# A hybrid encoder layer with a mixture of experts: bias fetches spread over the projection copies, w_ada units moved, and the last residual folded into the expert loop

## The chip, the cores and the metric

The program runs on one core of one Trainium2 chip. The metric is device time in microseconds (us) for one execution. Engines: TensorE (PE, matrix products; PEld its weight loads), VectorE (DVE), ScalarE (ACT), GpSimd (POOL), and the sync engine (SP), which here only issues DMAs. Every engine runs its own instruction list in order and waits on semaphores.

## The reference, cut to what matters

There are two groups of tokens, 256 prompt tokens and 32 sample tokens, and one layer:

```python
mod = jax.nn.silu(c) @ w_ada + b_ada                 # per group, 6 vectors of 1024
sh1, sc1, g1, sh2, sc2, g2 = jnp.split(mod[:, None, :], 6, axis=-1)
mix, state = mixer(x * (1.0 + sc1) + sh1)            # w_in projection, three head groups, w_out
x = layer_norm(DEEPNORM_ALPHA * x + g1 * mix, ln_g[0], ln_b[0])
ffn = moe_ffn(x * (1.0 + sc2) + sh2, w_router, b_router, w_e_in, b_e_in, w_e_out, b_e_out)
x = layer_norm(DEEPNORM_ALPHA * x + g2 * ffn, ln_g[1], ln_b[1])
```

`mixer` projects with `w_in` (1024 x 2048) into queries and keys of attention groups A and B, their values, and the two halves of a gated convolution (width 31, then LayerNorm and swish). Attention logits get a bias taken from a table by relative position. `moe_ffn` sends each token to 4 of 32 experts; each expert has 8 MB of `w_e_in` and 4 MB of `w_e_out` in f32, so the experts' weights are 384 MB. `DEEPNORM_ALPHA` is 2 ** 0.25.

## The kernel before, in words

All tokens lie in three tiles: `t` = 0 and 1 hold 128 prompt rows each, `t` = 2 the 32 sample rows, which for row-wise work are spread over 128 partitions as quarters of 256 columns (`x1q`).

**Front.** SP loads `w_ada` (six vectors, "pairs" 0 to 5, each in two halves, so twelve "units" of 2 MB) through a ring of four slots, and `w_in` behind the first four units. A unit from 4 on reuses a slot once TensorE has passed an earlier unit (`ada_done`). TensorE transposes `x`, does units 0 to 3 (`ada(u)`, L1429), then sixteen projection jobs, in the order gg0, ga0, gg1, ga1 (convolution), k0, k1, q0, q1, qb0 to qb3, kb, v0, v1, v2 (L1549, L1544, L1524, L1529). The jobs use two PSUM banks in turn, so job n waits until ScalarE has copied job n-2 out (`proj_used`). Table `ADA_AFTER` says behind which job each remaining `w_ada` unit is multiplied. Behind kb come the transposes of the convolution's output (`conv_rows`), behind v0 those of the new keys (three, L1478), the cached keys (L1486, L1490) and the convolution state (L1496). All transposes share two banks: transpose job j waits until VectorE has copied job j-2 (`tr_used`). VectorE meanwhile runs the convolution (L1006, L1010), its statistics (L1020), `add_mod` (L962, adds `b_ada` to a finished pair) and the copies (L1046). ScalarE writes finished pairs to DRAM (`store_mod`, L667), from where they are read back as rows.

The attention bias is built by GpSimd as a small table, stored by ScalarE into `ext_dram`, and fetched from there by ten DMAs that ScalarE issues in a row, before its first projection copy (L657 to L662; copy L675).

**Attention, output projection, LayerNorm, router** follow (logits L1576, exponentials L747, w_out L1660).

**Experts.** Tokens of an expert are taken in blocks of 32 slots; 51 blocks occur here. For each block TensorE gathers the token rows by one-hot products (L1773, L1774), multiplies with `w_e_in` (L1793), transposes, multiplies with `w_e_out` (L1822, semaphore `S2`), and adds the gated result of the block before to the sums in PSUM (`comb` and bank 7; `combine(0..2)`, L1756 and L1752). `combine(0)` of a block stands behind the gathers of the next. VectorE makes the one-hot picks (L1339, L1287 to L1291) and the activation (L1298 to L1306); ScalarE copies the second product to `outb` (L895) for `combine`. SP streams 1 MB pieces of expert weights (L415, L418) into a ring of 20 slots, each as soon as the product that used it has passed. Experts 0 and 1 are written out in line; experts 2 to 31 are a loop `Fori(0, 6)` on TensorE whose body holds five experts, each with an inner loop over its blocks. VectorE, ScalarE and SP have loops of their own over the same experts.

**End.** VectorE waits for the last `combine`, multiplies the sums with `g2` (L1365), adds `ALPHA` times `x1` (L1366; GpSimd has completed `x1` long before, L599 to L606, `x1_ready`), and does the last LayerNorm (L1371 to L1381). `g2` rows and the LayerNorm rows are loaded by SP behind the last expert weights.

## Time and profile before

| | us |
|---|---|
| runs of the kernel | 1264.98, 1255.98, 1263.4 (median 1263.4) |
| the profiled execution | 1256.61 |
| span of its trace | 1254.6 |
| TensorE busy in it | 1024.4 (82%) |
| VectorE busy | 317.2 (25%) |
| ScalarE busy | 179.4 (14%) |
| GpSimd busy | 64.5 (5%) |
| moved by DMA | 454.26 MB, 362 GB/s in the mean |

The profiled execution lies 6.8 us below the median of the runs, and its span 2.0 us below its own time. Busy shares are averages over stages with different limits; what a stage waits for is read from the rows of that stage.

### The profile page before, as it was taken

The numbers are of one execution on the slowest core, as the hardware profiler recorded it, in microseconds if no ns is written. First come the engines' busy times: TensorE is split into PE (matmuls) and PEld (weight loads), VectorE is DVE, ScalarE is ACT, GpSimd is POOL, SyncE is SP. The second block draws the span as 40 slices with busy tenths as digits, with TensorE's granted clock in tenths as the row PEclk, the third lists the DMA queues.
The fourth block names the chain that finished last, engine by engine and source line by source line (L and its number), as shares of the span: only waits on it lengthen the run. The fifth ranks groups of instructions, "written<-read, shape, count | busy, mean of one in ns | idle before, by whom it ended". The sixth has DMA issues, their size and how long they took to land.

```text
span 1254.6 us, 30804 instructions
## 1 busy us (share of the span) xinstructions
PE 1024.4 (82%) x12329; PEld 480.6 (38%) x12330; DVE 317.2 (25%) x1020; ACT 179.4 (14%) x522; POOL 64.5 (5%) x142
## 2 busy tenths in 40 slices
PE   2799897898989779779789968997878997876872
PEld 1556654344434324224334424442333442332431
DVE  0297556322213111102121211121121121211215
ACT  0101434211101101001011101111110110100110
POOL 1830000000051000000000000000000000000000
PEclk9999899899989879879899989998998998888996
DMA  9995875699999999997997997099799999999994
GB/s 338 338 337 219 219 291 202 262 421 419 422 420 421 419 421 421 421 421 312 420 421 321 421 420 293 32 422 420 332 410 420 376 378 420 422 419 421 421 420 149
DMA packets 77729, 454.26 MB, mean 362 GB/s; under 512 B 9060, under 2 KB 16446, under 8 KB 28426
## 3 DMA queue, kind: packets, MB, share of 16 engines
q1 hardware_dynamic: 73412, 448.53, 88.1%
q10 hardware_dynamic: 4229, 4.41, 1.1%
...
## 4 chain that ended last, share of the span: by engine, by line
PE 40%; DMA 25%; SPq 22%; DVE 7%; issue 5%; ACT 1%; DVEq 0%
DMA w<-in_w_e_out 24%; PE bank L1793 15%; SPq L415 10%; PE bank L1822 8%; SPq L418 7%; PE bank L1773 3%; SPq L396 3%; PE comb L1756 2%; PE bank L1660 1%; PE comb L1660 1%; PE bank L1810 1%; PE bank L1786 1%; DVE mt L1306 1%; DVE mt L1302 1%; DVE mt L1298 1%
## 5 line engine op out<-in xcount | busy, mean ns | idle before, releaser
L1793 PE MATMUL bank<-w,mt 128*32 128x512 f32 x3264 | 397.1, 630 | 47.6 <-DMA w<-in_w_e_in 47.6
L1822 PE MATMUL bank<-w,mt 128*32 128x256 f32 x3264 | 199.0, 389 | 48.5 <-DMA w<-in_w_e_out 34.0
L1793 PEld LDWEIGHTS bank<-w,mt 128*32 128x32 f32 x3264 | 96.7, 114 | 307.9 <-issue 212.7
L1298 DVE TENSOR_SCALAR mt<-bank 128x256 f32<-128x256 f32 x51 | 21.6, 424 | 698.8 <-PE bank L1793 698.8
L1822 PEld LDWEIGHTS bank<-w,mt 128*32 128x32 f32 x3264 | 98.6, 111 | 131.2 <-DMA w<-in_w_e_out 51.3
L1773 PE MATMUL bank<-pick,hb 128*128 128x32 bf16 x2448 | 79.6, 180 | 52.6 <-issue 52.3
L1773 PEld LDWEIGHTS bank<-pick,hb 128*128 128x128 bf16 x2448 | 75.3, 98 | 76.9 <-issue 76.5
L886 ACT ACTIVATE mt<-mt 128x256 f32<-128x256 f32 x51 | 21.3, 417 | 500.1 <-DVE mt L1298 500.1
L1756 PE MATMUL comb<-mt,gpickT 32*128 32x256 f32 x816 | 82.0, 476 | 0.5 <-ACT mt L895 0.5
L1774 PE MATMUL bank<-pick,hb 96*128 96x32 bf16 x408 | 72.8, 179 | 0.0
L1756 PEld LDWEIGHTS comb<-mt,gpickT 32*128 32x128 f32 x816 | 35.9, 206 | 51.3 <-issue 48.1
L895 ACT ACTIVATE mt<-bank 128x256 f32<-128x256 f32 x51 | 19.6, 384 | 237.6 <-PE bank L1822 237.6
L1774 PEld LDWEIGHTS bank<-pick,hb 96*128 96x128 bf16 x408 | 40.1, 98 | 0.0
L1810 PE MATMUL bank<-ident,mt 128*128 128x128 f32 x102 | 25.1, 328 | 16.0 <-DVE mt L1306 16.0
L1752 PE MATMUL bank<-mt,gpickT 128*128 128x256 f32 x102 | 38.1, 457 | 0.0
L1010 DVE SCALAR_TENSOR_TENSOR w<-w,cwT 128x318 f32<-128x318 f32 x60 | 36.7, 612 | 2.3 <-DVE mt L962 0.2
L1289 DVE TENSOR_SCALAR gpick<-iota,rkc,gtc 128x128 f32 (+1 forms) x102 | 34.6, 380 | 0.0
L1339 DVE TENSOR_SCALAR pick<-iota,rkc 128x32 bf16 x150 | 27.2, 246 | 20.1 <-DVE gtc L1327 10.8
L888 ACT ACTIVATE gpickT<-bank 128x384 f32<-128x384 f32 x51 | 25.0, 491 | 39.9 <-PE bank L1806 39.9
L1549 PE MATMUL comb<-mt,w 128*128 128x288 f32 x80 | 22.7, 439 | 5.9 <-ACT w L675 3.8
...
L1810 PEld LDWEIGHTS bank<-ident,mt 128*128 128x128 f32 x102 | 16.1, 206 | 26.4 <-DVE mt L1306 26.3
...
## 6 DMA issues: line engine op xcount, KB each, us to landing
w<-in_w_e_in SPq DMA_DIRECT2D x256, 1024.0 KB, 26.0
w<-in_w_e_out SPq DMA_DIRECT2D x128, 1024.0 KB, 21.5
...
```

Of the source, the lines that this page charges most:

```text
L396: sp.dma_start(win[:, :, a:b], wi[:, :, a:b]).then_inc(ld_win[piece], 16)
L415: sp.dma_start(slot[s], src).then_inc(ld_slot[s], 16)
L418: sp.dma_start(slot[s], src).then_inc(ld_slot[s], 16)
L1010: link(v.scalar_tensor_tensor(out=yconv[:, c, :], in0=uext[:, c, w:w + Y_LEN], scalar=cwT[:, c, w:w + 1], in1=yconv[:, c, :], op0=ALU.mult ...
L1289: v.tensor_scalar(gpick[:, t, :, :], ids, rkc[:, t, :], gtc[:, t, :], ALU.is_equal, ALU.mult)
L1752: return mm(bank[7][:, 0:256], gpickT[:, 2 * P:3 * P], outb, start=False, stop=True, skip_group_check=True)
L1756: ins = mm(comb[:, q, c:c + 256], gpickT[r, P * t:P * (t + 1)], outb[r, :], start=False, stop=True, skip_group_check=True)
L1773: mm(out, hb[:, HB_AT[t], h, P * k:P * (k + 1)], pick[:, t, :], start=(t == 0 and h == 0), stop=False)
L1774: ins = mm(out, hb_s[0:96, P * k:P * (k + 1)], pick[0:96, 2, :], start=False, stop=True)
L1793: ins = mm(quarter(bank[0][SLOTS * q:SLOTS * (q + 1), :], 0), xT[:, SLOTS * k:SLOTS * (k + 1)], quarter(slot[s], q), start=False, stop=(k ...
L1810: ins = nc.tensor.transpose(bank[6][:, 256 + P * c:256 + P * (c + 1)], act.rearrange("p (d k) -> p k d", k=2)[:, c, :], ident[:, :])
L1822: ins = mm(bank[0][SLOTS * q:SLOTS * (q + 1), 0:256], hid, slot[s][:, D * (k % 2) + 256 * q:D * (k % 2) + 256 * (q + 1)], start=False, sto ...
```

## The change

1. The ten bias fetches move from a row ahead of ScalarE's copies to places behind copies 0 to 5 (`fetch_bias`): one behind copy 0, one behind copy 1, two behind each of copies 2 to 5.
2. `w_ada` units 4 to 9 are multiplied one or so jobs later (`ADA_AFTER`), unit 10 between the new keys' transposes behind v0, unit 11 behind the convolution columns, just ahead of attention. Pair 5 goes to bank 7. The key transposes are split: new keys 0, 1, unit 10, new keys 2 and cached keys A behind v0; cached keys B and the convolution state behind v1. The swish's sigmoids on ScalarE move from behind v1 to behind v0. On VectorE the sinks' small operations move ahead and `add_mod(5)` behind the conv columns' copies; attention waits for pair 4 instead of 5 at its start, and for pair 5 before its first value product.
3. `g2` is loaded before the expert loop as two tiles of quarters (`g2q[0]` prompt, `g2q[1]` sample). VectorE writes the second product of each block times `g2` to `outb` and to `outb_s` (`scaled_rows`) instead of ScalarE's copy; `combine(2)` reads `outb_s`. `ALPHA * x1` is added by nine TensorE products with `ident_a` into the sums, after expert 6. For that, experts 2 to 6 are written out in line on TensorE, and its loop runs from 1 to 6. At the end VectorE takes statistics and the centred rows straight from PSUM; `total_rows` is gone.

```diff
-        ADA_AFTER = {5: 4, 6: 5, 8: 6, 9: 7, 11: 8, 12: 9, 13: 10, 14: 11}
+        ADA_AFTER = {6: 4, 7: 5, 9: 6, 10: 7, 11: 8, 12: 9}
+        ADA_BANKS = (0, 1, 0, 1, 0, 7)
...
+            for j in range(2):
+                src = bass.AP(tensor=mod_dram.tensor, offset=mod_dram.offset + (5 + 6 * j) * D, ap=[[256, 4], [0, 32], [1, 256]])
+                sp.dma_start(g2q[j], src).then_inc(ld["gain"], 16)
...
-            sp.dma_start(g2b, mod_dram[0:1, 5 * D:6 * D].to_broadcast([P, D])).then_inc(ld["gain"], 16)
-            sp.dma_start(g2q, quarters(mod_dram, 11 * D)).then_inc(ld["gain"], 16)
...
+            link(g.memset(ident_a[:, :], 0.0))
+            link(g.affine_select(out=ident_a[:, :], in_=ident_a[:, :], compare_op=ALU.not_equal, fill=ALPHA, base=0,
+                                 pattern=[[-1, P]], channel_multiplier=1))
...
-            eng.dma_start(bias_a, toeplitz(0, EXT_0 - 255, P, AH, 1, 256)).then_inc(ld["toep"], 16)
-            eng.dma_start(bias_b, toeplitz(AH, EXT_0 - 255, P, BH, 1, 256)).then_inc(ld["toep"], 16)
-            for i in range(4):
-                eng.dma_start(bias_sa[32 * i:32 * i + 32, :], bass.AP(tensor=ext_dram.tensor, offset=ext_dram.offset + i * EXT + EXT_0 - PAST - 31,
-                              ap=[[1, 32], [1, SA_K]])).then_inc(ld["toep"], 16)
-                eng.dma_start(bias_sb[32 * i:32 * i + 32, :, :], toeplitz(AH + i, EXT_0 - BCACHE - 31, 32, 2, 4, SB_K)).then_inc(ld["toep"], 16)
+            def fetch_bias(n):
+
+                if n == 0:
+                    eng.dma_start(bias_a, toeplitz(0, EXT_0 - 255, P, AH, 1, 256)).then_inc(ld["toep"], 16)
+                elif n == 1:
+                    eng.dma_start(bias_b, toeplitz(AH, EXT_0 - 255, P, BH, 1, 256)).then_inc(ld["toep"], 16)
+                else:
+                    i = n - 2
+                    eng.dma_start(bias_sa[32 * i:32 * i + 32, :], bass.AP(tensor=ext_dram.tensor, offset=ext_dram.offset + i * EXT + EXT_0 - PAST - 31,
+                                  ap=[[1, 32], [1, SA_K]])).then_inc(ld["toep"], 16)
+                    eng.dma_start(bias_sb[32 * i:32 * i + 32, :, :], toeplitz(AH + i, EXT_0 - BCACHE - 31, 32, 2, 4, SB_K)).then_inc(ld["toep"], 16)
 
...
+                if n < 6:
+                    fetch_bias(n)
                 if name == "qb0":
...
-                if name == "v1":
                     eng.wait_ge(conv_z, 1)
                     for c in range(3):
                         a.activation(zsig[0:TS[c], c, :], zrow[0:TS[c], c, :], ACT.Sigmoid).then_inc(conv_sig, 1)
...
-            for name in ("xT_a", "xT_b", "sig", "gT_copied", "aT", "out"):
+            for name in ("xT_a", "xT_b", "sig", "gT_copied", "aT"):
...
-                eng.wait_ge(m["S2"], n2)
-                a.activation(outb, bank[0][:, 0:256], ACT.Copy).then_inc(m["out"], 1)
...
-                ins = v.scalar_tensor_tensor(out=modr[:, pair % 2, :], in0=bank[pair % 2][:, 0:256], scalar=one,
+                ins = v.scalar_tensor_tensor(out=modr[:, pair % 2, :], in0=bank[ADA_BANKS[pair]][:, 0:256], scalar=one,
...
+            dve.wait_ge(ld["sinks"], 16)
+            link(v.tensor_scalar(nsink[:, :], nsink[:, :], -1.0, None, ALU.mult))
+            for i in range(4):
+                r = slice(32 * i, 32 * i + 32)
+                link(v.tensor_copy(nsink_s[r, :], nsink[r, :].rearrange("p (n i) -> p i n", n=2)[:, i, :]))
...
-            add_mod(5)
...
-            dve.wait_ge(ld["sinks"], 16)
-            link(v.tensor_scalar(nsink[:, :], nsink[:, :], -1.0, None, ALU.mult))
-            for i in range(4):
-                r = slice(32 * i, 32 * i + 32)
-                link(v.tensor_copy(nsink_s[r, :], nsink[r, :].rearrange("p (n i) -> p i n", n=2)[:, i, :]))
+            add_mod(5)
...
+            def scaled_rows(n):
+
+                dve.wait_ge(m["S2"], n)
+                v.tensor_tensor(outb, bank[0][:, 0:256], g2q[0], ALU.mult).then_inc(m["out"], 1)
+                v.tensor_tensor(outb_s, bank[0][:, 0:256], g2q[1], ALU.mult).then_inc(m["out_s"], 1)
...
                     ins.then_inc(m["pick"], 1)
+                    scaled_rows(n1)
                     gated_picks(bass.ds(first, SLOTS), n2)
                     activate(n1, n2)
...
+            dve.wait_ge(ld["gain"], 2 * 16)
...
-            def total_rows(t):
-
-                if t == 2:
-                    dst, y, gain, tmp = x1q, bank[7][:, 0:256], g2q, ytmp_s
-                    dve.wait_ge(fin_c, 2)
-                else:
-                    c = slice(256 * t, 256 * t + 256)
-                    dst, y, gain = XY[:, t, :], comb[:, :, c], g2b.rearrange("p (b x) -> p b x", b=4)
-                    tmp = ytmp[t]
-                    dve.wait_ge(fin_c, 1)
-                dve.wait_ge(x1_ready, t + 1)
-                link(v.tensor_tensor(tmp if t == 2 else tmp.rearrange("p (b x) -> p b x", b=4), y, gain, ALU.mult))
-                link(v.scalar_tensor_tensor(out=dst, in0=dst, scalar=ALPHA, in1=tmp, op0=ALU.mult, op1=ALU.add))
+            scaled_rows(dve.snap(dve.value_load(cum[0:1, NE + 2:NE + 3], min_val=32, max_val=160) + 1, min_val=33, max_val=161))
+
+            def total(t):
+
+                return bank[7][:, 0:256] if t == 2 else comb[:, :, 256 * t:256 * t + 256]
 
             def statistics(t):
 
                 for j in range(2):
-                    link(v.bn_stats(bnst[:, j, :], XY[:, t, 512 * j:512 * (j + 1)]))
+                    link(v.bn_stats(bnst[:, j, :], total(t)[:, 2 * j:2 * j + 2, :]))
                 link(v.bn_aggr(cstat[:, t, :], bnst[:, :, :]))
                 root(t)
 
             def centred(t, dst, gain):
 
-                link(v.scalar_tensor_tensor(out=dst, in0=dst, scalar=cstat[:, t, 0:1], in1=gain, op0=ALU.subtract, op1=ALU.mult))
+                if t < 2:
+                    dst, gain = (x.rearrange("p (b x) -> p b x", b=4) for x in (dst, gain))
+                link(v.scalar_tensor_tensor(out=dst, in0=total(t), scalar=cstat[:, t, 0:1], in1=gain, op0=ALU.subtract, op1=ALU.mult))
 
             def scaled(t, dst, shift):
 
                 v.scalar_tensor_tensor(out=dst, in0=dst, scalar=cstd[:, t:t + 1], in1=shift, op0=ALU.mult, op1=ALU.add).then_inc(fin_ready, 1)
 
-            dve.wait_ge(ld["gain"], 2 * 16)
-            total_rows(0)
-            total_rows(2)
-            link(v.bn_stats(bnst_s, x1q))
-            v.tensor_tensor(spread, bnst_s.unsqueeze(1).to_broadcast([P, 4, 6]), qmask[:, :].unsqueeze(2).to_broadcast([P, 4, 6]), ALU.mult)             .then_inc(fin_stats, 1)
+            dve.wait_ge(fin_c, 2)
+            link(v.bn_stats(bnst_s, total(2)))
+            v.tensor_tensor(spread, bnst_s.unsqueeze(1).to_broadcast([P, 4, 6]), qmask[:, :].unsqueeze(2).to_broadcast([P, 4, 6]), ALU.mult)\
+             .then_inc(fin_stats, 1)
             statistics(0)
             dve.wait_ge(ld["final"], 4 * 16)
             centred(0, XY[:, 0, :], lng2)
...
             dve.wait_ge(fin_spread, 1)
             link(v.bn_aggr(cstat[:, 2, :], bank[5][:, 0:24].rearrange("p (q s) -> p q s", q=4)))
             root(2)
-            total_rows(1)
...
-                        ins = mm(bank[pair % 2][32 * j:32 * j + 32, 0:256], scT[:, k, :], ring[:, ada_slot(u), q, 256 * j:256 * (j + 1)],
+                        ins = mm(bank[ADA_BANKS[pair]][32 * j:32 * j + 32, 0:256], scT[:, k, :], ring[:, ada_slot(u), q, 256 * j:256 * (j + 1)],
...
-                    new_keys()
-                    cached_keys()
+                    new_keys(0)
+                    new_keys(1)
+                    ada(10)
+                    new_keys(2)
+                    cached_keys("A")
+                elif name == "v1":
+                    cached_keys("B")
                     conv_state()
             conv_columns()
-
-
+            ada(11)
...
-                    pe.wait_ge(mod_ready, 6)
+                    pe.wait_ge(mod_ready, 5)
...
+                if s == 0:
+                    pe.wait_ge(mod_ready, 6)
...
-                    return mm(bank[7][:, 0:256], gpickT[:, 2 * P:3 * P], outb, start=False, stop=True, skip_group_check=True)
+                    return mm(bank[7][:, 0:256], gpickT[:, 2 * P:3 * P], outb_s, start=False, stop=True, skip_group_check=True)
...
                     pe.wait_ge(m["out"], n1)
                     combine(0)
+                    pe.wait_ge(m["out_s"], n1)
...
-            with pe.Fori(0, NE // 5) as i:
+            for e in range(2, 7):
+                moe(e % 5, e, {t: 16 * t for t in range(1, 6)} if e < 5 else {t: 16 * (t + 3) for t in range(1, 3)}, *block_range(pe, e))
+            pe.wait_ge(x1_ready, 3)
+            for t in range(2):
+                for q in range(4):
+                    mm(comb[:, q, 256 * t:256 * t + 256], ident_a[:, :], XY[:, t, 256 * q:256 * q + 256], start=False, stop=True, skip_group_check=True)
+            mm(bank[7][:, 0:256], ident_a[:, :], x1q, start=False, stop=True, skip_group_check=True)
+            with pe.Fori(1, NE // 5) as i:
...
-            pe.wait_ge(m["out"], total)
+            pe.wait_ge(m["out_s"], total)
```

TensorE around the first `w_ada` units behind the projection; an L1549 or L1544 row is a projection job (k0 is the first row), an L1429 row is a `w_ada` unit. Before, and then in the changed kernel, where the same rows are L1560, L1555 and L1438:

```order
L1549 MATMUL comb<-mt,w 128x288 x8
L1549 MATMUL bank<-mt,w 128x288 x8
L1429 MATMUL bank<-w,scT 32x256 x16
L1549 MATMUL comb<-mt,w 128x288 x8
L1429 MATMUL bank<-w,scT 32x256 x16
L1549 MATMUL bank<-mt,w 128x288 x8
L1544 MATMUL comb<-mt,w 64x288 x16
```

```order
L1560 MATMUL comb<-mt,w 128x288 x8
L1560 MATMUL bank<-mt,w 128x288 x8
L1560 MATMUL comb<-mt,w 128x288 x8
L1438 MATMUL bank<-w,scT 32x256 x16
L1560 MATMUL bank<-mt,w 128x288 x8
L1438 MATMUL bank<-w,scT 32x256 x16
L1555 MATMUL comb<-mt,w 64x288 x16
```

Units 4 and 5 stand one job later: q0 is now ahead of unit 4, and q1 ahead of unit 5.

TensorE from v0 (two rows, L1524, in the changed kernel L1535) to the last row ahead of attention's first logits. L1478 and L1488 are the new keys, L1486 and L1498 cached keys A, L1490 and L1500 cached keys B, L1496 and L1507 the convolution state, L1504 and L1515 the convolution columns. Before, then changed:

```order
L1429 MATMUL comb<-w,scT 32x256 x16
L1478 MATMUL comb<-ident,w 128x128 x6
L1478 MATMUL comb<-ident,w 32x128 x3
L1486 MATMUL comb<-ident,w 128x128 x4
L1490 MATMUL comb<-ident,w 128x128
L1496 MATMUL comb<-ident,w 30x128 x4
L1524 MATMUL comb<-w,mt 128x256 x8
L1524 MATMUL comb<-w,mt 128x128 x8
L1429 MATMUL comb<-w,scT 32x256 x16
L1529 MATMUL bank<-w,mt 32x128 x24
L1504 MATMUL comb<-ident,hb 128x128 x4
L1508 MATMUL comb<-ident,hb 128x32 x2
```

```order
L1488 MATMUL comb<-ident,w 128x128 x6
L1438 MATMUL bank<-w,scT 32x256 x16
L1488 MATMUL comb<-ident,w 32x128 x3
L1498 MATMUL comb<-ident,w 128x128 x4
L1535 MATMUL comb<-w,mt 128x256 x8
L1535 MATMUL comb<-w,mt 128x128 x8
L1500 MATMUL comb<-ident,w 128x128
L1507 MATMUL comb<-ident,w 30x128 x4
L1540 MATMUL bank<-w,mt 32x128 x24
L1515 MATMUL comb<-ident,hb 128x128 x4
L1519 MATMUL comb<-ident,hb 128x32 x2
L1438 MATMUL bank<-w,scT 32x256 x16
```

Units 10 and 11 are the two L1429 (L1438) rows: unit 10 goes from ahead of the key transposes to between them, unit 11 from ahead of v2 to just ahead of those logits, and the two last transpose jobs go behind v1.

VectorE in the body of a block loop: `pick` and `gpick` are the one-hot tiles, the rows from `bank` to `mt` the activation. Before, then changed:

```order
L1339 TENSOR_SCALAR pick<-iota,rkc 128x32 x2
L1339 TENSOR_SCALAR pick<-iota,rkc 96x32
L1287 TENSOR_SCALAR gpick<-iota,rkc,gtc 128x128
L1289 TENSOR_SCALAR gpick<-iota,rkc,gtc 128x128 x2
L1290 REGISTER_ALU
L1291 TENSOR_TENSOR gpick<-gpick,qmask 128x128
L1298 TENSOR_SCALAR mt<-bank 128x256
L1299 TENSOR_SCALAR mt<-bank 128x256
L1302 SCALAR_TENSOR_TENSOR mt<-mt 128x256
L1306 TENSOR_TENSOR mt<-mt 128x256
```

```order
L1354 TENSOR_SCALAR pick<-iota,rkc 128x32 x2
L1354 TENSOR_SCALAR pick<-iota,rkc 96x32
L1306 TENSOR_TENSOR mt<-bank,xy 128x256
L1307 TENSOR_TENSOR xy<-bank,xy 128x256
L1296 TENSOR_SCALAR gpick<-iota,rkc,gtc 128x128
L1298 TENSOR_SCALAR gpick<-iota,rkc,gtc 128x128 x2
L1299 REGISTER_ALU
L1300 TENSOR_TENSOR gpick<-gpick,qmask 128x128
L1313 TENSOR_SCALAR mt<-bank 128x256
L1314 TENSOR_SCALAR mt<-bank 128x256
L1317 SCALAR_TENSOR_TENSOR mt<-mt 128x256
L1321 TENSOR_TENSOR mt<-mt 128x256
```

The two products with `g2` (L1306, L1307 of the changed kernel) stand between the picks and the gated picks.

## Rows read from the trace of the kernel before

**Rows 1.** The page: DMA busy in tenths, slices of 31.4 us; chain of waits by engine.

```profile
...
DMA  9995875699999999997997997099799999999994
...
PE 40%; DMA 25%; SPq 22%; DVE 7%; issue 5%; ACT 1%; DVEq 0%
```

**Rows 2.** Timeline, ScalarE, 41 to 52 us: start, length, instruction, [idle before and its releaser].

```profile
...
50.63 0.41 ACT L675 ACTIVATE w<-comb 128x288 f32<-128x288 f32 x1 [10.57 <-issue]
```

**Rows 3.** Timeline of TensorE, 36 to 80 us, same columns.

```profile
...
51.09 5.84 PE L1549 MATMUL comb<-mt,w 128*128 128x288 f32 x16 [3.81 <-ACT w L675]
...
64.53 4.04 PE L1549 MATMUL bank<-mt,w 128*128 128x288 f32 x16
70.44 1.93 PE L1429 MATMUL bank<-w,scT 128*32 128x256 f32 x32 [1.88 <-DMA w<-in_w_ada]
72.31 4.15 PE L1549 MATMUL comb<-mt,w 128*128 128x288 f32 x16
```

**Rows 4.** 51.1 to 57 us: PE, PEld, DVE, ACT, POOL busy; granted clock 0.71; DMA.

```profile
...
51.10:57.00 5.90, 5.90 (x17) 4.39 (x18) 1.80 (x2) 0.45 (x3) 5.63 (x5) 0.71 1.07 329
```

**Rows 5.** Timeline, 60 to 135 us, from the convolution's statistics to the first logits.

```profile
...
110.60 0.43 DVE L1020 BATCH_NORM_STATS2 bnst<-comb 128x6 f32<-128x256 f32 x1 [4.12 <-PE comb L1466]
...
119.58 1.26 DVE L1046 COPY w<-comb 128x384 f32<-128x384 f32 x2 [0.17 <-DVE mt L970]
...
120.20 0.50 PE L1478 MATMUL comb<-ident,w 128*32 128x128 f32 x3 [1.58 <-DVE w L1046]
...
133.72 1.28 ACT L704 ACT_TABLE_LOAD   x1 [0.94 <-issue]
...
133.83 0.68 PE L1576 MATMUL comb<-w,anti 128*128 128x128 f32 x4 [1.12 <-DVE mt L1070]
```

**Rows 6.** Timeline of all engines, 135 to 160 us, first softmax.

```profile
...
135.76 0.37 ACT L747 ACTIVATE hb<-comb,stat 128x128 f32<-128x128 f32 x1 [0.55 <-issue]
...
138.03 0.16 DVE L1110 RECIPROCAL rinv<-esum 128x2 f32<-128x2 f32 x1
```

**Rows 7.** Timeline of TensorE, 415 to 445 us.

```profile
...
422.67 0.32 PE L1773 MATMUL bank<-pick,hb 128*128 128x32 bf16 x6 [7.32 <-issue]
```

**Rows 8.** Chain that ended last, 430 to 600 us, in order of time.

```profile
...
442.88 28.49 DMA w<-in_w_e_out
...
595.47 6.95 issue
```

**Rows 9.** The page: costliest groups, the combine product of the sample rows.

```profile
...
L1752 PE MATMUL bank<-mt,gpickT 128*128 128x256 f32 x102 | 38.1, 457 | 0.0
```

**Rows 10.** Timeline of GpSimd, 200 to 420 us, its last work.

```profile
...
377.82 4.79 POOL L602 TENSOR_TENSOR xy<-xy,mt 128x1024 f32<-128x1024 f32 x2
```

**Rows 11.** Timeline, 784.5 to 792 us, one block ending, the next beginning.

```profile
...
785.73 3.66 PE L1822 MATMUL bank<-w,mt 128*32 128x256 f32 x64 [0.25 <-ACT mt L891]
...
789.45 0.39 ACT L895 ACTIVATE mt<-bank 128x256 f32<-128x256 f32 x1 [3.78 <-PE bank L1822]
...
790.81 0.71 PE L1756 MATMUL comb<-mt,gpickT 32*128 32x256 f32 x8
```

**Rows 12.** Groups by line, VectorE, 1232 to 1255 us: xcount | busy, mean ns | idle.

```profile
...
L1366 DVE SCALAR_TENSOR_TENSOR xy<-xy,w 128x1024 f32<-128x1024 f32 (+1 forms) x3 | 2.9, 958 | 0.1
...
L1365 DVE TENSOR_TENSOR w<-comb,w 128x1024 f32<-128x1024 f32 x2 | 2.4, 1224 | 12.5 <-PE comb L1756 12.5
...
L1365 DVE TENSOR_TENSOR w<-bank,w 128x256 f32<-128x256 f32 x1 | 0.4, 426 | 0.0
```

**Rows 13.** Timeline of all engines, 1200 to 1255 us, the end.

```profile
...
1232.24 0.38 ACT L895 ACTIVATE mt<-bank 128x256 f32<-128x256 f32 x1 [8.89 <-PE bank L1822]
...
1232.68 2.09 PE L1756 MATMUL comb<-mt,gpickT 32*128 32x256 f32 x16 [0.50 <-ACT mt L895]
...
1234.70 1.22 PE L1752 MATMUL bank<-mt,gpickT 128*128 128x256 f32 x2
1234.90 1.22 DVE L1365 TENSOR_TENSOR w<-comb,w 128x1024 f32<-128x1024 f32 x1 [12.52 <-PE comb L1756]
```

44 lines of the change are left out of this document (22 added, 22 removed).

## The prediction

> **What bounds the kernel now.** I read the page first, then the waits and the timeline of each stretch. The chain of waits is shared by TensorE (40%), DMA (25%) and SP's issuing (22%) [rows 1]. The DMA line shows why: from slice 9 on the DMA engines are full except in slices such as the 26th (0 tenths), where the ring of 20 weight slots is full and TensorE works through one expert's blocks. So the expert part is a relay: a full DMA stretch, then a TensorE stretch, and what shortens only the side that is not carrying the chain is lost. Ahead of the experts there is a front of some 200 us set by TensorE and its waits, and behind them a tail of some 20 us on VectorE alone. The profiled execution took 1256.6 us; 1% of this kernel, 12.6 us, is about what a measurement can tell from no change. The three runs shown spread over 9.0 us, so I work out a difference within the profiled execution and take it off the median, 1263.4.
>
> **Bias fetches behind the copies.** ScalarE does its first projection copy at 50.63 only, after issuing the ten fetches [rows 2], and TensorE stood 3.81 us for it; the job behind took 5.84 us instead of 4.04, at a granted clock of 0.71 [rows 3, 4]. Put behind the copies, both go: copy 0 can run when job 0 ends, near 43.4, and jobs then follow each other at 3.9 us (64.53 + 4.04 and its predecessors). But the next thing late is known: unit 4 of `w_ada` lands at 70.44 [rows 3]. Jobs 2 to 5 end 5.6 us earlier, at about 63, q0 fills the next 3.9, and TensorE waits again from about 66.6 to 70.44, 3.8 us. What is really gained here is that q0, which stood behind unit 4, is now under that wait: 4.1 us (the job at 72.31) [rows 3]. Two terms stand against each other. The new wait is as long as the old one, which was followed by a slower clock and 1.8 us lost (5.84 less 4.04); the wait of 1.88 us ahead of 70.44 cost nothing: the unit behind it took 1.93 us, as all later ones do [rows 3]. And unit 4 may land earlier, since 1 MB of bias rows no longer competes with `w_in` at 43 us; the trace shows no case of that, I bound it by 0 and by 2 us. With 1 us of it the wait is 2.8 us, halfway between the two rows, so 0.9 us for the clock. The two cancel: front so far -4.1, bounds -2.3 (all of the clock, nothing earlier) and -6.1.
>
> **Keys, value products, units 10 and 11.** From conv_rows on, VectorE's chain is the same length: from 110.60 (statistics) to the first key copy at 119.58 is 9.0 us, and TensorE stood 1.58 us for it at the third key transpose [rows 5]. All of this moves up by 4.1. Moving unit 10 between the transposes leaves TensorE waiting there as before: the third transpose starts at about 116.1 against 120.20, so the splitting by itself gains nothing. Then v1 follows at once, cached keys B and the convolution state run behind it, v2 ends near 125.9, and VectorE (state copy 0.7, sinks 0.9, three products 1.1) lets the conv columns go near 126.8. Unit 11 (1.9 us) now covers the wait of 1.12 us in which TensorE stood for VectorE's last copies [rows 5]. First logits: about 129.6 against 133.83, -4.2. Here a new wait arises: `add_mod(5)` cannot start before unit 11 ends, ScalarE's four stores of pair 5 (1.2 us) and its table load (1.28 us) [rows 5] stand behind it, so the first exponential comes at 132.9 against 135.76, only -2.8 [rows 6]. What counts is VectorE's first normalisation, at 138.03 behind three maxima [rows 6]; the maxima end at about 134.0 and the exponentials at 133.8, so it starts at 134.0: -4.0. If the exponentials set it after all, -2.8. The two added `g2` loads cost SP about 1.2 us of issuing; the first expert weights behind them are used 70 us later, so nothing. Front: -4.0.
>
> **Does it pass through the experts?** Every load of the first experts is released by an event on TensorE or VectorE, so the relay begins 4 us sooner as a whole. I take 4.0, with 0 as the far bound.
>
> **In the loop.** VectorE's two products with `g2` have the form of L1365 out of bank 7, 0.43 us each [rows 12]. In a TensorE-bound block the second product ends at 785.73 + 3.66 = 789.39, and the combine that reads `outb` starts at 790.81, 1.42 us later, because the gathers lie between [rows 11]. VectorE's first product ends about 0.5 us behind 789.39, the second 0.9; TensorE needs the second only behind combine(0), at 791.5. Cover 0.9 and 1.2 us, cost nothing. The gated picks slide 1.6 us later but are used behind the whole next first product, some 9 us on. One more wait instruction on TensorE a block: nothing that I can see. ScalarE's 0.39 us [rows 11] was not on the path. GpSimd finished `x1` at 382.6 [rows 10], and TensorE asks for it at about 411, so that wait is free. Nine products with `ident_a`: 457 ns for each instruction of the same shape [rows 9], two a product, overlapping, 4 to 8 us at one place.
>
> **The unrolled experts.** At 415.35 TensorE stopped for 7.32 us ahead of expert 7 with nothing to wait for [rows 7]; another stands at 595.47 (6.95) [rows 8], five such in all, and a loop of six passes jumps back five times. An ordinary change of expert costs 0.6. Written out, the first of them goes: 6.7 us less, 4 to 8 us more for `ident_a`, at the same place. There the chain runs in SP's issues and then in a DMA piece of 28.49 us from 442.88 to 471.4 [rows 8], in slices where DMA is full [rows 1], and TensorE is the one that waits. So both are worth nothing. The Trainium skill says of this ("Runtime: NRT & Kernel Launch", Instruction fetch mechanics) that prefetch is sequential, and a taken branch outside the held pages stalls until the target is fetched, which is why kernels prefer to be unrolled. The trace agrees on the stall, 7.3 us; by that rule alone the sum would be 6.7 us better, and the rows of the chain say that it is not.
>
> **The tail.** Gone are the products of L1365 and L1366: 2.4 + 0.4 + 2.9 = 5.7 us busy [rows 12], some 0.2 more in gaps, 5.9, all on the chain. Added: VectorE makes both `outb` tiles before the last combine, 0.9 us where ScalarE's copy took 0.38, so TensorE starts near 1233.15 instead of 1232.68, +0.5; and VectorE waits for `combine(2)` as well, which ended at 1234.70 + 1.22 = 1235.92, where before it started at 1234.90 behind `combine(1)` [rows 13], so +1.1. Reading PSUM instead of SBUF costs nothing: 1024 columns took 1224 ns from PSUM (L1365) and (2.9 - 0.4) / 2 = 1.25 us from SBUF (L1366) [rows 12]. The LayerNorm rows are asked for 1.6 us earlier, but 0.6 MB of `g2` no longer lies ahead of them. Tail: -5.9 + 1.6 = -4.3; bounds -3.5 and -5.
>
> **Sum.** -4.0 - 4.3 = -8.3: 1263.4 - 8.3 = **1255.1 us** (1248.3 against the profiled 1256.6).
>
> **Rivals.** (a) The front's gain is taken back on the way, by a load or the first exponentials; only the tail is left: -4.3, 1259.1. For it: the expert part is half DMA; against: it was never ahead of TensorE at its beginning. 18%. (b) The jump back taken away does pay, with unit 4 early too: -8.3 - 2.6 (6.7 less 4.1) - 2.0 = -12.9, 1250.5. For it the 7.32 us; against it the chain. 12%. (c) Slower: VectorE's row products come too late for the combine. This decides from 0.9 us behind `S2` on; the picks that stand ahead of them in VectorE's list end 4 us before `S2` within an expert and 0.2 to 0.7 us before it where the expert changes. Were both products bare in the some 30 blocks whose second product runs unbroken, 30 x 0.86 = 26 us: 1281. 4%. (d) The new wait for unit 4 takes the full clock loss and the exponentials set attention's start: -8.3 + 1.8 + 1.2 = -5.3, 1258.1; this lies inside my forecast's own range, 1252 to 1259.
>
> **How the numbers follow.** Forecast with (d) 66%, (a) 18%, (b) 12%, (c) 4%. Eight in ten lie between (b) and (a), widened by the scatter of three runs (half of 9.0 us about): 1247 to 1262. Faster by over 1% needs -12.6, that is (b) and a part of the forecast helped by scatter: 0.17. Slower by over 1%: (c), 0.04. Within 1%: 0.79.
>
> **What would show it.** Right: no ScalarE wait ahead of job 2; TensorE waiting for `w_ada` from about 67 to 70; first logits near 129.6 and first normalisation near 134; no stop of 7 us near 410, four left; the combine 1.4 us behind the second product as before; the last VectorE instruction some 15.5 us behind the last expert product instead of 19.9. Wrong: a `w_ada` wait longer than 4 us or a second one at units 8 or 9 (issued 9.7 us before use); a combine later than 1.5 us; the DMA-full stretches beginning no sooner than before.

## The result, and the profile after

The changed kernel took 1247.31 us (median of 5 runs, 1246.47 to 1250.04) beside 1260.79 us for the kernel before (5 runs, 1255.98 to 1264.98): ratio 0.9896, 95% interval 0.9865 to 0.9927. I had forecast 1255.1. The later sittings, with many more runs of the kernel before, give it 1256.23 (35 runs), 1257.58 (12) and 1256.53 us (17), and the changed program once more gave 1246.73 us, ratio 0.9922 [0.9896, 0.9947]. So the change is worth some 10 us, between 6.7 (by 0.9947) and 17 (by 0.9865), and the 1263.4 us from which I subtracted was a high median of three.

The page of the profiled execution (1250.0 us, span 1248.3), the lines that answer to [rows 1] and to the costliest groups:

```profile
...
DMA  9987685699999999997997998099989989999995
...
PE 40%; DMA 25%; SPq 23%; DVE 6%; issue 5%; ACT 1%; DVEq 0%
...
L1790 PE MATMUL bank<-pick,hb 128*128 128x32 bf16 x2448 | 79.4, 179 | 45.2 <-issue 44.9
...
```

The picture is the same: full DMA, one empty slice near 780 to 810 us, the same shares of the chain. The timeline of TensorE, projections (before: [rows 3]):

```profile
...
59.87 4.04 PE L1560 MATMUL bank<-mt,w 128*128 128x288 f32 x16
63.75 4.04 PE L1560 MATMUL comb<-mt,w 128*128 128x288 f32 x16
70.86 3.64 PE L1438 MATMUL bank<-w,scT 128*32 128x256 f32 x32 [3.06 <-DMA w<-in_w_ada]
74.43 5.26 PE L1560 MATMUL bank<-mt,w 128*128 128x288 f32 x16
```

The wait for ScalarE is gone, and the jobs follow each other at 3.88 us. TensorE then stands 3.06 us for unit 4, which lands at 70.86. Behind that wait the unit takes 3.64 us instead of 1.93 and the job 5.26 instead of 4.15, 2.8 us in all. The windows view shows the granted clock there (the third number from the end), 0.50 of full, which is 1.2 of 2.4 GHz:

```profile
...
66.00:70.00 4.00, 1.80 (x8) 1.08 (x6) 3.93 (x3) 0.41 (x1) 3.86 (x3) 0.99 1.04 369
70.00:74.00 4.00, 3.14 (x32) 1.39 (x32) 3.82 (x6) 0.00 (x0) 2.78 (x5) 0.50 1.04 383
74.00:78.00 4.00, 4.00 (x18) 2.72 (x11) 3.75 (x8) 0.00 (x0) 0.00 (x0) 0.66 0.84 231
...
```

All engines, from the key transposes to the first softmax (before: [rows 5, 6]):

```profile
...
119.35 0.50 PE L1488 MATMUL comb<-ident,w 128*32 128x128 f32 x3 [1.73 <-DVE w L1055]
...
120.61 7.09 PE L1535 MATMUL comb<-w,mt 128*128 128x256 f32 x32
...
134.02 0.71 PE L1591 MATMUL comb<-w,anti 128*128 128x128 f32 x4
...
137.35 0.37 ACT L758 ACTIVATE hb<-comb,stat 128x128 f32<-128x128 f32 x1
...
138.25 0.16 DVE L1119 RECIPROCAL rinv<-esum 128x2 f32<-128x2 f32 x1
```

In this execution the front has gained nothing: the first normalisation stands at 138.25 against 138.03. The value product v1 took 7.09 us where before it took 5.40, again at a lower granted clock (0.52 from 121 to 123 us, 0.63 from 123 to 125). In the expert loop, the place where TensorE stopped 7.32 us before [rows 7]:

```profile
...
412.71 3.66 PE L1840 MATMUL bank<-w,mt 128*32 128x256 f32 x64 [0.25 <-ACT mt L902]
416.31 3.72 PE L1862 MATMUL comb<-xy,ident_a 128*128 128x256 f32 x16
...
420.30 0.30 PE L1790 MATMUL bank<-pick,hb 128*128 128x32 bf16 x6
```

The stop is gone; the products with `ident_a` took its place. Other stops stay: the chain names three, 7.01 us at 596.48, 7.09 at 936.45 and 6.91 at 1097.96. A fourth, 7.39 us up to 736.34, is not on it. A block bound by TensorE (before: [rows 11]):

```profile
...
786.91 3.66 PE L1840 MATMUL bank<-w,mt 128*32 128x256 f32 x64 [0.25 <-ACT mt L902]
...
790.98 0.41 DVE L1307 TENSOR_TENSOR xy<-bank,xy 128x256 f32<-128x256 f32 x1
...
792.00 0.71 PE L1773 MATMUL comb<-mt,gpickT 32*128 32x256 f32 x8
```

VectorE's second product ends at 791.39, the combine starts at 792.00, 1.43 us behind the expert product's end: the new products are covered. The tail (before: [rows 13]):

```profile
...
1230.80 1.07 PE L1840 MATMUL bank<-w,mt 128*32 128x256 f32 x16 [1.64 <-DMA w<-in_w_e_out]
1231.94 0.42 DVE L1306 TENSOR_TENSOR mt<-bank,xy 128x256 f32<-128x256 f32 x1 [7.51 <-PE bank L1840]
1232.28 0.41 DVE L1307 TENSOR_TENSOR xy<-bank,xy 128x256 f32<-128x256 f32 x1
...
1232.75 1.15 PE L1773 MATMUL comb<-mt,gpickT 32*128 32x256 f32 x16 [0.88 <-DVE xy L1307]
...
1233.83 0.70 PE L1769 MATMUL bank<-xy,gpickT 128*128 128x256 f32 x2
1234.56 0.43 DVE L1395 BATCH_NORM_STATS2 cwT<-bank 128x6 f32<-128x256 f32 x1 [1.87 <-PE bank L1769]
...
1244.37 1.41 DVE L1392 SCALAR_TENSOR_TENSOR xy<-xy,cstd,w 128x512 f32<-128x512 f32 x2
```

VectorE's last instruction ends at 1245.78, 13.91 us behind the last expert product (19.9 before): 6.0 us, where I had 4.3. So in this profile the tail makes nearly all of the 6.3 us between the spans (1254.6 and 1248.3), and the timed difference is larger. That asks what the front is worth, and how much one execution can tell of it.

### The profile page after: what moved, and what is told of

Its sections match the earlier page's. It is cut to its first block, busy times and chain, and to the rows that moved or that the text cites. A ratio compares the mean times of both kernels' runs of the same rounds, so it can differ in the third digit from the quotient of the medians.

```text
span 1248.3 us, 30883 instructions
## 1 busy us (share of the span) xinstructions
PE 1022.7 (82%) x12347; PEld 484.4 (39%) x12348; DVE 350.1 (28%) x1116; ACT 162.9 (13%) x471; POOL 65.3 (5%) x144
## 4 chain that ended last, share of the span: by engine, by line
PE 40%; DMA 25%; SPq 23%; DVE 6%; issue 5%; ACT 1%; DVEq 0%
DMA w<-in_w_e_out 24%; PE bank L1811 15%; SPq L416 11%; PE bank L1840 8%; SPq L419 7%; PE bank L1790 3%; SPq L397 3%; PE comb L1773 2%; PE bank L1677 1%; PE comb L1677 1%; DMA w<-in_w_ada 1%; PE bank L1828 1%; PE bank L1438 1%; PE bank L1804 1%; DVE mt L1321 1%
## 5 line engine op out<-in xcount | busy, mean ns | idle before, releaser
L1306 DVE TENSOR_TENSOR mt<-bank,xy 128x256 f32<-128x256 f32 x51 | 21.7, 425 | 145.0 <-PE bank L1840 144.9
L892 ACT ACTIVATE mt<-bank 128x128 f32<-128x128 f32 x51 | 14.1, 277 | 274.5 <-PE bank L1791 274.5
L1019 DVE SCALAR_TENSOR_TENSOR w<-w,cwT 128x318 f32<-128x318 f32 x60 | 39.8, 663 | 2.2
L1769 PE MATMUL bank<-xy,gpickT 128*128 128x256 f32 x102 | 37.4, 449 | 0.0
L1298 DVE TENSOR_SCALAR gpick<-iota,rkc,gtc 128x128 f32 (+1 forms) x102 | 30.5, 343 | 0.0
```

The costliest lines, as they stand in the source:

```text
L1019: link(v.scalar_tensor_tensor(out=yconv[:, c, :], in0=uext[:, c, w:w + Y_LEN], scalar=cwT[:, c, w:w + 1], in1=yconv[:, c, :], op0=ALU.mult ...
L1298: v.tensor_scalar(gpick[:, t, :, :], ids, rkc[:, t, :], gtc[:, t, :], ALU.is_equal, ALU.mult)
L1769: return mm(bank[7][:, 0:256], gpickT[:, 2 * P:3 * P], outb_s, start=False, stop=True, skip_group_check=True)
```

## The experiments

All times are read against the kernel before, run beside them on the same chip.

**The two halves.** front_only is the change down to the attention (fetches, key transposes, `w_ada` units), tail_only the rest (factor and residual in the loop, unrolled experts, shorter tail).

```diff
 front_only, out of the change (with the moved key transposes):
-        ADA_AFTER = {5: 4, 6: 5, 8: 6, 9: 7, 11: 8, 12: 9, 13: 10, 14: 11}
+        ADA_AFTER = {6: 4, 7: 5, 9: 6, 10: 7, 11: 8, 12: 9}
...
+                if n < 6:
+                    fetch_bias(n)
 tail_only, out of the change (with the row products behind each expert product):
-            with pe.Fori(0, NE // 5) as i:
+            with pe.Fori(1, NE // 5) as i:
```

> Parts 1 and 2 of the change alone (bias fetches, units, key transposes), the end and the loop as before; like all experiment kernels it loads the two loop ends with stated bounds, which costs nothing that counts. In the profile after, TensorE waited 3.06 us for unit 4 and then ran at a lower clock, and ScalarE's first exponential came 1.6 us later than before. Theory A (the front gives back in clock and in a ScalarE queue what the moved job gains): ratio to before 0.999 to 1.002, first exponential at 136 to 138 us. Theory B (that loss belongs to the one profiled execution): -4 us, ratio 0.997.

> Part 3 alone (products with g2 on VectorE in the loop, ALPHA x1 on TensorE, experts 2 to 6 in line, shorter end), the front as before. Theory A (all that is gained is in the last stretch, 6.0 us from the last expert product to VectorE's last instruction): -6 us, ratio 0.995. Theory C (the loop gains as well, since the timed medians differ by 13.5 us and the end explains 6): -10 to -13 us, ratio 0.990 to 0.992.

front_only: 1253.61 us, ratio 0.9963 [0.9942, 0.9985], -4.6 us; first gather of the experts at 221.68 (223.75 before). The first exponential came at 136.32, as theory A had it, but the time is that of theory B. The trace has only 2.1 us of the 4.6. tail_only: 1250.29 us, ratio 0.9954 [0.9924, 0.9984], -5.8 us, theory A; its trace ends 15.37 us behind the last expert product. The product of the ratios is 0.9917, -10.4 us. That agrees with the 0.9922 of the whole change (the control, below), and neither half's interval holds 1: each is worth something. The tail of tail_only differs from that of the changed kernel in TensorE's two combines:

```profile
...
1231.26 2.09 PE L1758 MATMUL comb<-mt,gpickT 32*128 32x256 f32 x16 [0.86 <-DVE xy L1300]
...
1233.28 1.22 PE L1754 MATMUL bank<-xy,gpickT 128*128 128x256 f32 x2
1234.54 0.43 DVE L1388 BATCH_NORM_STATS2 cwT<-bank 128x6 f32<-128x256 f32 x1 [3.33 <-PE bank L1754]
```

2.09 and 1.22 us as before [rows 13], at a granted clock of 0.50 from 1230 us on; the changed kernel's 1.15 and 0.70 ran at 1.00. That is the whole 1.46 us between 15.37 and 13.91. Of the nine traces with the new tail four show 13.9 and five 15.4 us, and both happen to the same program with small edits far away.

**The fetches alone.**

```diff
 bias_only: before, with
-            eng.dma_start(bias_a, toeplitz(...)).then_inc(ld["toep"], 16)
...
                 ins.then_inc(proj_used, 1)
+                if n < 6:
+                    fetch_bias(n)
```

> The kernel before with the bias fetches behind the projection copies and nothing else. Jobs 2 to 5 then end near 63 us and unit 4 of w_ada, which still stands behind job 5, lands near 70.5. Theory A (the wait only moves, and a longer wait costs more clock): a wait of 7 us, then a lower clock for 2.8 us lost against the kernel before, +1 to +3 us, ratio 1.001 to 1.002. Theory B (no clock loss, weights come earlier without the fetches ahead of them): -1 to -2 us, ratio 0.999.

1258.65 us, 1.0023 [1.0000, 1.0047]: theory A, no gain, if anything a loss. TensorE's timeline:

```profile
...
58.77 4.04 PE L1556 MATMUL bank<-mt,w 128*128 128x288 f32 x16
70.68 3.64 PE L1436 MATMUL bank<-w,scT 128*32 128x256 f32 x32 [7.87 <-DMA w<-in_w_ada]
74.25 4.68 PE L1556 MATMUL comb<-mt,w 128*128 128x288 f32 x16
```

The wait taken away at job 2 comes back, longer, at unit 4 (7.87 us), and with the lower clock behind it.

**The units a job later.** Added to bias_only, and taken away from the changed kernel. Only units 4 to 7 are moved by it; 8 and 9 stand behind the same jobs in all these kernels:

```diff
 bias_later: bias_only, and
-        ADA_AFTER = {5: 4, 6: 5, 8: 6, 9: 7, 11: 8, 12: 9, 13: 10, 14: 11}
+        ADA_AFTER = {6: 4, 7: 5, 9: 6, 10: 7, 11: 8, 12: 9, 13: 10, 14: 11}
 ada_early: the changed kernel, and
-        ADA_AFTER = {6: 4, 7: 5, 9: 6, 10: 7, 11: 8, 12: 9}
+        ADA_AFTER = {5: 4, 6: 5, 8: 6, 9: 7, 11: 8, 12: 9}
```

> The kernel before with the bias fetches behind the copies, as in bias_only (1.0023), and units 4 to 7 of w_ada a job later besides. Theory A (the step of my prediction: what is gained at w_ada is that the job of 4.1 us which stood behind unit 4 now runs while unit 4 is on its way): the wait for unit 4 falls from the 7.87 us of bias_only to about 3 us; the first gather of the experts comes 2 to 5 us earlier than in bias_only (223.59), at 219 to 222, and the time is 0.997 to 0.999 of before. Theory B (the copies and the key chain behind set the time whatever stands at w_ada): the first gather stays near 223.6, ratio 1.000 to 1.003.

> The changed kernel with units 4 to 9 of w_ada back where they stood before. Theory A (the job later is worth what it puts under the wait): the wait for unit 4 becomes 7 to 8 us again, TensorE's clock is lower behind it, and the first gather comes 3 to 5 us later than in the control kernel (221.04), at 224 to 226; time 3 to 5 us over the control, 0.995 to 0.997 of before. Theory B (the first gather stays within 1.5 us of the control's, since its own spread, 221.0 and 224.8 in two executions of the same program, is made elsewhere): ratio as the control, 0.992.

bias_later: 1252.05 us, 0.9962 [0.9943, 0.9981]; wait for unit 4 of 4.17 us, first gather 220.10. That is as good as front_only (0.9963), which has the reordered keys besides: those bring nothing that can be measured. ada_early: 1251.28 us, 0.9960 [0.9943, 0.9978], some 4.8 us above the control by the ratios; wait 5.96 us, first gather 223.90. Theory A holds from both sides, though the waits missed its numbers (4.17 us for 3, 5.96 for 7 to 8): the fetches bring nothing until the later units find a use for the time that they free. The third case, the units moved with the fetches left in a row, was not run. In the kernel before, 1.88 us of waiting for unit 4 stood there for a job to fill, so some part of the gain may not need the fetches.

**The control**, the changed kernel with two block bounds read by another form of the same load, as in all these kernels:

```diff
-                eng.reg_load(ends[e + 1], cum[0:1, e + 3:e + 4])
+                ends[e + 1] = eng.value_load(cum[0:1, e + 3:e + 4], min_val=1, max_val=160)
```

> The changed kernel once more, with only the first two block bounds read into registers by the other form of the same load that all experiments use. Nothing in it should move the time: both theories expect 0.990 to 0.992 of the kernel before, 1245 to 1248 us beside 1256 to 1259. It is the base for the other three runs. If the scatter of the kernel before made the first result (0.9896) too large, it comes out nearer to 0.993, the 8.3 us that I had forecast; the product of the two parts measured alone (0.9963 and 0.9954) is 0.9917.

0.9922, as expected. Its first gather came at 221.04 where the first profile of the changed kernel had 224.84. Of these 3.8 us, 2.7 arise at unit 4: here TensorE waited 2.60 us for it, and the unit took 1.93 us and kept the full clock. They are still 2.8 at the first normalisation; the other 1.0 us comes behind it.

```profile
...
64.29 4.04 PE L1560 MATMUL comb<-mt,w 128*128 128x288 f32 x16
70.94 1.93 PE L1438 MATMUL bank<-w,scT 128*32 128x256 f32 x32 [2.60 <-DMA w<-in_w_ada]
```

**The wait for unit 4, and the exponentials.**

```diff
 rows_behind_ada: the changed kernel, SP's list
-            (loads of ln_g, ln_b, conv_ln_g, conv_ln_b, cached keys, sinks)
             for u in range(4, 12):
                 ada_unit(u)
                 if u == 5:
+                    (the same loads)
 exp_early: the changed kernel, ScalarE's list
-            store_mod(5, 3)
             a.activation(warm[0:1, 0:1], warm[0:1, 1:2], ACT.Exp)
+            store_mod(5, 3)
 rows_exp: both
```

> The changed kernel with SP's small row loads (layer norm rows, cached keys, sinks) issued behind the loads of w_ada's units 4 and 5 instead of ahead of them. Theory A (the wait of 3.06 us for unit 4 on TensorE at 67.8, and the lower clock behind it: 3.64 us instead of 1.93 for the unit, 5.26 instead of 4.0 for the job behind it, 7.09 instead of 5.40 for the second value product, are one cost, all caused by how late unit 4 is issued): with unit 4 issued 2 to 3 us earlier the wait goes below 1 us and the full clock stays; first logits and first gather come 3 to 6 us earlier, and the time falls by 3 to 6 us against the control. Theory B (the copies on ScalarE and the exponentials set attention's start anyway): first logits move by up to 1 us, time 0 to -1. Theory C (unit 4 is late because w_ada's bytes arrive at the rate of the queue, not because of its issue): the wait stays at about 3 us, and nothing moves.

> The changed kernel with ScalarE's table load for the exponential one step earlier, ahead of its last store of a modulation row. Theory A (in the changed kernel the exponentials, not the logits, set when attention starts: logits 134.0, table load 135.8, first exponential 137.4): the first exponential comes 1.1 to 1.4 us earlier, and all behind it too, so the time falls by 1 to 1.3 us against the control. Theory B (attention's start is not on the path; what follows is bound by TensorE's own row of work): the first exponential moves and the first gather of the experts (224.84 in the changed kernel) does not, change 0.

> The changed kernel with both earlier edits of the front together: SP's small rows behind units 4 and 5, and ScalarE's table load one step earlier. In rows_behind_ada the table load stood at 130.66 behind four stores of 1.15 us, first exponential 132.17, first normalisation 133.07. Theory A (the exponentials are then the last to come): first normalisation near 132, first gather 1 us earlier than its 217.26, span 1241, ratio 0.989 to 0.991. Theory B (VectorE's maxima, done at 132.8, hold the first normalisation at 133): nothing moves against rows_behind_ada (1242.0 span, ratio 0.9914).

rows_behind_ada: 1245.08 us, 0.9914 [0.9889, 0.9939]. SP issued unit 4 at 47.57 instead of 58.46; TensorE doesn't wait for it:

```profile
...
62.97 4.04 PE L1560 MATMUL comb<-mt,w 128*128 128x288 f32 x16
66.95 1.93 PE L1438 MATMUL bank<-w,scT 128*32 128x256 f32 x32
68.81 4.15 PE L1560 MATMUL bank<-mt,w 128*128 128x288 f32 x16
```

The first normalisation comes at 133.07, the first gather at 217.26, 3.8 us ahead of the control's, and the span is 3.0 shorter. C, that the rate of the queue sets the wait for unit 4, falls. Of theory A half is left. Further on TensorE stands again, for unit 6 and for a copy that waits behind ScalarE's stores:

```profile
...
83.68 1.93 PE L1438 MATMUL comb<-w,scT 128*32 128x256 f32 x32 [0.95 <-DMA w<-in_w_ada]
...
93.65 4.10 PE L1555 MATMUL bank<-mt,w 128*64 128x288 f32 x32 [2.14 <-ACT w L699]
```

So of 4.0 us gained on the control at unit 4, 0.8 are left at v0 (106.20 against 106.96). Another 1.7 us arise by the first normalisation, 1.4 of them at v1, which ran at full clock here and not in the control; the last 1.4 come behind it. The timed ratio moved by only -0.0008 with intervals of 0.0025 to either side, so in the times this gain is not shown.

exp_early: 1247.04 us, 0.9919 [0.9895, 0.9942], no change. It moved the first exponential to 1.9 us behind the first logits (3.3 in the control) and left the first normalisation 4.24 us behind them (4.23). In all_three below the table load is early as well, and the normalisation stands at 133.03, as in rows_behind_ada without it. VectorE's maxima set it, not the exponentials: theory A falls, and theory B of rows_exp holds. rows_exp: 1245.43 us, 0.9910 [0.9887, 0.9933], as rows_behind_ada; there v1 ran 6.80 us instead of 5.40, which puts its normalisation at 134.60 and not at 133.

**The jumps back.** The first pass of TensorE's loop written out in the kernel before, and then the whole loop in the changed one:

```diff
 inline_only (before)             all_in_line (changed)
-    with pe.Fori(0, NE // 5) as i:
+    for e in range(2, 7):
+        moe(e % 5, e, {...}, *block_range(pe, e))
+    with pe.Fori(1, NE // 5) as i:
 and in all_in_line
-    with pe.Fori(1, NE // 5) as i:
+    for i in range(1, NE // 5):
```

> The kernel before with nothing changed but experts 2 to 6 written out in line on TensorE. Theory A (the jump back taken away lay in a stretch that the DMA bounds): 0 us, ratio 0.999 to 1.001, and the stop of 7 us near 415 us gone with the next expert's weights still late. Theory D (a jump taken away is worth its length): -6.7 us, ratio 0.995.

> The changed kernel with TensorE's loop over the experts written out: no jump back is left on it. Theory A (the stops of about 7 us behind each jump back, at 596, 728, 936 and 1098, are paid in full where TensorE is the bound, and only the first one, in the stretch bound by transfers, was worth nothing): three of the four are on the chain that ended last and each is 6.4 to 6.7 us longer than an ordinary step between two experts, so the time falls by 17 to 20 us against the control, to about 0.976 of the kernel before. Theory B (the queue of weight loads is the bound everywhere in the experts' stretch and each stop only lets the loads run ahead): 0 to -3 us. Theory C (straight code has to be fetched as well and brings short stops of its own, more of them than the loop had): 0 or slower, with waits of over 1 us for nothing at many experts on TensorE.

inline_only: 1256.92 us, 1.0006 [0.9980, 1.0033]. The stop ahead of expert 7 went:

```profile
...
415.94 0.30 PE L1773 MATMUL bank<-pick,hb 128*128 128x32 bf16 x6 [0.83 <-issue]
```

But the run is no clean test of that stop. Behind each of the four stops that were left a new one of 3.2 to 3.6 us appeared, which neither the kernel before nor any other one here has. Three of them are on the chain that ended last; one pair of it:

```profile
...
1095.49 6.96 issue
...
1102.88 3.56 issue
...
```

In sum TensorE stood still longer in this kernel than before, by some 7 us (6.5 taken away, 13.5 new), and the time did not move. Why the new stops came is not shown. all_in_line has no stop left and is the clean test: 1248.09 us, 0.9926 [0.9893, 0.9959], the same as the control to within some 5 us. My theory A, 17 to 20 us, falls. The waits view of TensorE (total us, times, longest), first of the control, then of all_in_line:

```profile
...
PE bank L1811 <- DMA w<-in_w_e_in: 50.4, 50, 2.7
PE bank L1790 <- issue: 45.6, 30, 7.3
PE bank L1840 <- DMA w<-in_w_e_out: 30.1, 26, 1.5
...
```

```profile
...
PE bank L1811 <- DMA w<-in_w_e_in: 70.0, 67, 2.9
PE bank L1840 <- DMA w<-in_w_e_out: 37.8, 31, 2.8
PE bank L1790 <- issue: 16.4, 28, 1.0
...
```

All stops are gone, 29.2 us of them, and 27.3 us have come back as waits for expert weights: TensorE got to its products earlier and stood there for the DMA. The second number is rough, since the same waits sum to 80.5 us in the control and 89.4 in the first profile of the changed kernel. Three of these stops stand on the chain that ended last, in the control as in the first profile of the changed kernel, and still taking them away gave nothing that the times show.

```diff
 all_three: rows_exp, and
-    with pe.Fori(1, NE // 5) as i:
+    for i in range(1, NE // 5):
```

> The changed kernel with all three: small rows behind w_ada, early table load, and TensorE's loop over the experts written out. From the runs so far I expect that the stretch from the first gather to the last expert product keeps its 1006.5 to 1009 us whatever is taken off TensorE in it, so this one ends where rows_exp ends, span 1239 to 1242, ratio 0.989 to 0.991. The rival (the stops at the jumps back begin to count once the front is shorter) gives a stretch below 1005 us.

1245.80 us, 0.9908 [0.9886, 0.9930], the ratio as expected; the span of 1244.5 us missed my 1239 to 1242. From first gather to last expert product it took 1009.4 us, above my 1006.5 to 1009 and far from the 1005 of the rival, which falls too. It, rows_exp and rows_behind_ada are the best kernels of this study, each 1 to 2 us under the control by the ratios, which the intervals do not settle.

**One table over the traces**: start of v0; VectorE's first normalisation; first gather of the experts; end of the last expert product; the stretch between the last two; VectorE's end behind the last expert product; the execution's span.

| kernel | v0 | normalisation | gather | last product | stretch | tail | span |
|---|---|---|---|---|---|---|---|
| before | 110.54 | 138.03 | 223.75 | 1232.18 | 1008.4 | 19.9 | 1254.6 |
| bias_only | 113.02 | 140.51 | 223.59 | 1231.53 | 1007.9 | 19.9 | 1253.9 |
| inline_only | 110.83 | 138.32 | 222.77 | 1231.82 | 1009.1 | 19.9 | 1254.2 |
| front_only | 108.74 | 137.22 | 221.68 | 1230.73 | 1009.1 | 19.9 | 1253.1 |
| bias_later | 108.47 | 137.25 | 220.10 | 1228.17 | 1008.1 | 19.7 | 1250.3 |
| tail_only | 110.20 | 137.69 | 223.39 | 1230.40 | 1007.0 | 15.4 | 1248.3 |
| changed | 109.70 | 138.25 | 224.84 | 1231.87 | 1007.0 | 13.9 | 1248.3 |
| control | 106.96 | 135.49 | 221.04 | 1228.54 | 1007.5 | 13.9 | 1245.0 |
| exp_early | 108.54 | 137.09 | 221.55 | 1230.42 | 1008.9 | 15.4 | 1248.3 |
| ada_early | 113.22 | 140.09 | 223.90 | 1231.30 | 1007.4 | 15.4 | 1249.2 |
| all_in_line | 108.59 | 135.46 | 219.54 | 1226.10 | 1006.6 | 15.4 | 1244.0 |
| rows_behind_ada | 106.20 | 133.07 | 217.26 | 1224.12 | 1006.9 | 15.4 | 1242.0 |
| rows_exp | 106.06 | 134.60 | 219.08 | 1226.56 | 1007.5 | 13.9 | 1243.0 |
| all_three | 106.17 | 133.03 | 218.74 | 1228.12 | 1009.4 | 13.9 | 1244.5 |

The stretch keeps 1006.6 to 1009.4 us whatever is done in front of it or to TensorE in it (1007.6 in the mean of the nine kernels with the new loop, 1008.5 in the other five). The gather moves by 7.6 us, and the last product moves with it. But not all of that is made by the edits: from the first normalisation to the first gather, where the edits change next to nothing, the traces take between 82.9 us (bias_later) and 86.6 (changed). What decides it is not shown, so the gather of one execution tells an edit's worth to some 2 us only; v0 and the normalisation tell it better.

## Why the prediction was right or wrong

The forecast, no more than 1% gained and -8.3 us, had the mechanisms right, and -8.3 lies inside the control's interval (6.7 to 13.1 us). Timed alone, the front was worth 4.6 us (1.9 to 7.3) against my 4.0, the tail 5.8 (2.0 to 9.5) against my 4.3, so the times fault neither term. The traces do: they show less of the front than I took and more of the tail, and that the sum is so near is in part luck.

**Bias fetches behind the copies.** Right in its structure: the wait at job 2 goes, a new one comes at unit 4 (3.06 us, forecast 2.8 to 3.8), and what is gained is the job now run under it; bias_only, bias_later and ada_early show this from three sides. What failed is the step in which the two small terms cancel, 0.9 us of clock against 1 us of earlier landing. Unit 4 was used at 70.68 to 71.07 us in the eight traces with the moved fetches and SP's old order, and at 70.10 to 70.73 in the three with the old fetches (before, inline_only, tail_only): some 0.5 us later, not 1 us earlier. The clock cost not 0.9 but 2.8 us (1.71 at the unit, 1.11 at the job) in the profiled execution, nothing in the control, and 1.6 in each of the other four traces with both edits and the old order (front_only, bias_later, exp_early, all_in_line). So in the start of v0 the front so far was -0.8 us in the profile and -3.6 in the control against the 110.54 of before; the mean of the six is 108.50 against 110.52 for the three old fronts, -2.0. I had -4.1, bounds -2.3 and -6.1: five of the six traces gained less than my lower bound. The mean closes by terms: -4.1 + 1.6 + 0.5 = -2.0. The sign "a `w_ada` wait longer than 4 us" came up too, by a little (4.17 in bias_later, 4.08 in exp_early).

**Keys and value products.** "The splitting by itself gains nothing" is right: front_only and bias_later time alike. Unit 11 covers the copies as said: at full clock the way from v0 to the first logits is 22.6 us (rows_behind_ada, all_three) against 23.3 before, better than my 0.1. But v1 ran at the lower clock in six of the eleven traces with the new front or a part of it (6.3 to 7.1 us, bias_later among them, so it isn't the reordered keys that bring it), and then the way is 24.3. I had not counted that; before, v1 took 5.40. First logits near 129.6 and a first normalisation near 134, my signs of being right, came in none of the six: logits at 131.2 to 134.0, normalisation at 135.5 to 138.3, in the mean -1.2 us against the old fronts (136.79 and 138.01) where I had -4.0. At the first gather it is -1.8 (221.46 and 223.30). Only the kernels with SP's new order reach my numbers (133.03 to 134.60). Against these 1 to 2 us the times give the front 4.6 and, in bias_later, 4.8 us, with 1.9 as the nearest bound. The gap is not explained. That the maxima, and not the exponentials, set the first normalisation is right: 4.23 us behind the first logits, with or without the early table load. With that the second half of rival (d) falls; its first half, the full clock loss, came in the profiled execution and not in the control.

**Does it pass through the experts?** In full, as I took it, to the 1.4 us either way by which the stretch itself scatters: the end of the last product follows the gather down the table. Rival (a) (18%) falls with that and with front_only, whose interval does not hold 1.

**In the loop, and the unrolled experts.** Both at nothing, and right: 1.43 us between product and combine (forecast 1.42), `ident_a` 4.0 us where I had 4 to 8, four stops left. all_in_line is the direct answer to rival (b): written-out code avoids the stop (at expert 7, 0.83 us instead of 7.32 in inline_only; nothing over 1.0 us in all_in_line), and the time did not move. The Trainium skill ("Runtime: NRT & Kernel Launch", Instruction fetch mechanics) gives this stall as a reason to unroll. The traces agree on the stop at each jump back, 6.8 to 7.6 us; that unrolling pays they do not show here. My expectation for all_in_line then went wrong on the point that I had got right once. I read the three stops on the chain as stops in a stretch bound by TensorE. The page of the profile had the answer: in the slices of 596, 936 and 1098 us the DMA line stands at 9 tenths, and the only empty slice, 780 to 811 us, has no stop in it. The windows view of just these three stops gives a DMA share of 1.02 in each (421 to 426 GB/s). Rival (c), a late VectorE, did not come: in the profile after, TensorE's combines waited 0.9 us for the new products in all, at the tail.

**The tail.** By terms: the products of [rows 12] gone, -5.94 us (forecast -5.9: VectorE from its first instruction behind the combine to its end, 17.17 us before, 11.23 in tail_only). The later start cost +1.42 (forecast +1.6). Together -4.5 us, as in five of nine traces. The rest, up to -6.0, is TensorE's clock at the combine, 0.50 or 1.00. I gave no term to that; timed, the tail made 5.8 with an interval of 2.0 to 9.5, so the times don't settle which it mostly is. Over all traces the sum is -1.8 at the gather, -0.9 in the stretch and -5.2 in the tail, -7.9 us where the control's ratio gives -9.8.

**The base.** I took the difference off 1263.4 us, a median of three. Later medians of the same kernel lie at 1256.2 to 1257.6. Of the 7.8 us between 1255.1 and 1247.3, 2.6 is that base against the 1260.8 beside which the change was first timed, and 5.2 is the difference itself, measured as 13.5 in that sitting, while the control's ratio gives 9.8 and the two halves 10.4.

**Left open.** What decides the clock behind a short wait is not shown by these runs; nor why the front is worth more in the times than in the traces, what the later units are worth without the moved fetches, and whether SP's order (rows_behind_ada) pays in the times.
